# Choosing 256 keys by a threshold built bit by bit, in place of rounds of eight

## The reference

```python
def indexer_scores(qi, wi, ki):
    s = jnp.einsum('bqhd,bsd->bqhs', qi, ki).astype(jnp.float32)
    return jnp.einsum('bqhs,bqh->bqs', jax.nn.relu(s), wi.astype(jnp.float32)) * (IDX_DIM ** -0.5 * IDX_HEADS ** -0.5)

sc = jnp.where((key_chunk[None, :] <= q_chunk[:, None])[None], sc, -jnp.inf)
_, idx = lax.top_k(sc, k_sel)            # k_sel = 256 (80 for the sample)
valid = (idx // CHUNK) <= q_chunk[None, :, None]
return selected_attention(qblk, gather_rows(k, idx), gather_rows(v, idx), valid)
```

## Time and profile before

| | |
|---|---|
| time, median of 3 runs | 2787.55 us (2786.24 to 2788.78) |
| profiled execution, its span | 2790.9 us |
| PE busy | 2646.1 us (95%) |
| DVE busy | 1546.9 us (55%) |
| ACT busy | 922.8 us (33%) |
| POOL busy | 175.6 us (6%) |
| all MAX8 (202) | 170.9 us |
| all MATCH_REPLACE8 (202) | 172.1 us |

### The profile page before, as it was taken

How to read it: one execution, slowest core, us unless ns; L and a number is a source line. 1 busy time by engine, 2 the same in 40 slices (tenths; PEclk the granted TensorE clock), 3 DMA queues, 4 the chain that set the end, 5 groups by cost and what they waited for, 6 DMA issues and landing times. The chain is left out here.

```text
span 2790.9 us, 36346 instructions
## 1 busy us (share of the span) xinstructions
PE 2646.1 (95%) x14198; PEld 2323.7 (83%) x14198; DVE 1546.9 (55%) x2793; ACT 922.8 (33%) x1762; POOL 175.6 (6%) x168
## 2 busy tenths in 40 slices
PE   7999999999999999979969988899999999999996
PEld 6778789989899999868757777887898999999895
DVE  2445363444444444566889799963634444444535
ACT  3207343323222222322044555562532222223231
POOL 0300040000000000300020000000400000000003
PEclk9999999999999999989965898899999999999998
DMA  4110311101010101131100000003110101011011
GB/s 136 46 41 1 115 49 45 61 30 60 30 60 30 60 30 45 61 94 31 44 8 1 1 1 1 1 30 121 59 46 31 60 30 59 31 42 48 30 46 65
DMA packets 81279, 124.25 MB, mean 45 GB/s; under 512 B 6224, under 2 KB 54736, under 8 KB 81168
## 3 DMA queue, kind: packets, MB, share of 16 engines
q1 hardware_dynamic: 81168, 122.74, 13.4%
HBM read 110.98 MB, written 11.75 MB: 44 GB/s over the span
## 5 line engine op out<-in xcount | busy, mean ns | idle before, releaser
L1213 PE MATMUL psum<-xt_hi,layer_w_hi 128*128 128x384 f32 (+1 forms) x1536 | 505.5, 329 | 3.2 <-DVE xt_lo L847 3.2
L1215 PE MATMUL psum<-xt_hi,layer_w_lo 128*128 128x384 f32 (+1 forms) x1536 | 505.0, 329 | 0.0
L1214 PE MATMUL psum<-xt_lo,layer_w_hi 128*128 128x384 f32 (+1 forms) x1536 | 504.9, 329 | 0.0
L1128 DVE TENSOR_TENSOR act<-psum,act 128x512 f32<-128x512 f32 x540 | 366.2, 689 | 233.6 <-PE psum L1251 230.7
L1249 PE MATMUL psum<-layer_w_hi,layer_h_split 128*128 128x512 f32 x1024 | 400.0, 391 | 2.8 <-DVE layer_h_split L1116 1.6
L1250 PE MATMUL psum<-layer_w_lo,layer_h_split 128*128 128x512 f32 x1024 | 399.3, 390 | 0.0
L1251 PE MATMUL psum<-layer_w_hi,layer_h_split 128*128 128x512 f32 x1024 | 399.1, 390 | 0.0
L1116 DVE TENSOR_TENSOR layer_h_split<-layer_h_raw,layer_h_split 128x384 fp32r<-128x384 f32 (+1 forms) x192 | 98.4, 512 | 352.8 <-ACT layer_h_split L1029 352.8
L1213 PEld LDWEIGHTS psum<-xt_hi,layer_w_hi 128*128 128x128 f32 x1536 | 288.3, 188 | 4.7 <-DVE xt_lo L847 3.5
L1214 PEld LDWEIGHTS psum<-xt_lo,layer_w_hi 128*128 128x128 f32 x1536 | 288.4, 188 | 1.3
L1215 PEld LDWEIGHTS psum<-xt_hi,layer_w_lo 128*128 128x128 f32 x1536 | 288.4, 188 | 0.0
(11 more groups left out here) (215 smaller groups left out, 4067.5 us busy)
## 6 DMA issues: line engine op xcount, KB each, us to landing
layer_w_raw<-in_ff_w SPq DMA_DIRECT2D x64, 1024.0 KB, 6.3
ab_in_w_raw<-in_ab_w_in SPq DMA_DIRECT2D x12, 512.0 KB, 4.5
c_in_w_raw<-in_c_w_in SPq DMA_DIRECT2D x12, 512.0 KB, 3.9
ab_in_xt_raw<-in_xT SPq DMA_DIRECT2D x8, 512.0 KB, 4.2
layer_resid<-in_x SPq DMA_DIRECT2D x16, 256.0 KB, 2.8
x_scratch<-act SPq DMA_DIRECT2D x8, 512.0 KB, 2.6
layer_resid<-x_scratch SPq DMA_DIRECT2D x16, 256.0 KB, 2.7
out_y_prompt<-act SPq DMA_DIRECT2D x8, 512.0 KB, 2.6
```

Source lines behind the costliest of these rows:

```text
L1128: dve.tensor_tensor(acc, banks[4 + g % 4][0:r], acc, ALU.add).then_inc(y_read, 1)
L1213: pe.matmul(out, w1_hi[:, k, w], xt_hi[:, k, a:b], start=(k == 0), stop=False)
L1214: pe.matmul(out, w1_hi[:, k, w], xt_lo[:, k, a:b], start=False, stop=False)
L1215: mm = pe.matmul(out, w1_lo[:, k, w], xt_hi[:, k, a:b], start=False, stop=(k == KT - 1))
```

## The change

For tiles 7 to 2 (m = 1 to 6) the 256th largest score is found as a threshold, bit by bit from bit 30 down, and the mask is made by comparing with it. The sample keeps its rounds of eight. A first pass counts the scores that are at least 0; where a query has fewer than 256, its row's signs are flipped, so that the threshold is positive. Each of 31 further passes counts the scores at or above the threshold so far (`tensor_scalar` with `accum_out`, its elementwise output going to a spare buffer); the sign of the count's excess says whether the bit tried last stays, and two instructions on one column, bitwise ones, drop it or not and set the next bit. The tables that place the rounds are the same: 32 finds and marks for each tile at the same heads. `close` becomes longer: signs are restored, scores above the threshold are counted, those equal to it are numbered by a running sum, and as many of them as are still missing are kept. All later rounds wait for a close, which uses both spare buffers. `spare` takes 2 x 1024 fp32 per partition next to the score buffers; the program's scratch for dynamic DMA is set to 4096 in exchange. `MASKED` becomes a power of two.

```diff
-MASKED = -1e30
+MASKED = -(2.0 ** 100)
...
+def counted(m):
+
+    return C_RANKED[m] < SAMPLE
...
+        spare = top.take("ranking_spare", [P, 2, SEQ])
+        found = {m: 0 for m in range(len(C_RANKED))}
...
+    def row(self, m, n):
+
+        return self.eight(m)[:, n:n + 1]
+
+    def after(self, dve, m):
+
+        if max(self.last.get(m, 0), self.closed):
+            dve.wait_ge(self.chain, max(self.last.get(m, 0), self.closed))
+
     def find(self, dve, ranks):
 
         for m in ranks:
-            if m in self.last:
-                dve.wait_ge(self.chain, self.last[m])
-            self.step(m, dve.max(self.eight(m), self.scored(m)))
+            self.after(dve, m)
+            x = self.scored(m)
+            if not counted(m):
+                self.step(m, dve.max(self.eight(m), x))
+                continue
+            r, nk = x.shape
+            excess, short, _, threshold = [self.row(m, n) for n in range(4)]
+            ones = self.spare[0:r, m % 2, 0:nk]
+            if self.found[m] == 0:
+                self.step(m, dve.tensor_scalar(ones, x, 0.0, 0.5 - TOPK, ALU.is_ge, ALU.add, accum_out=excess))
+            else:
+                self.step(m, dve.tensor_scalar(ones, x, threshold, short, ALU.is_ge, ALU.add, accum_out=excess))
 
     def mark(self, dve, ranks):
 
         for m in ranks:
-            dve.wait_ge(self.chain, self.last[m])
-            self.step(m, dve.match_replace(self.scored(m), self.eight(m), self.scored(m), TAKEN))
+            x = self.scored(m)
+            self.after(dve, m)
+            if not counted(m):
+                self.step(m, dve.match_replace(x, self.eight(m), x, TAKEN))
+                continue
+            nk = x.shape[1]
+            excess, short, sign, threshold, dropped = [self.row(m, n) for n in range(5)]
+            if self.found[m] == 0:
+                dve.memset(threshold, 2.0)
+                self.step(m, dve.tensor_scalar(short, excess, 0.0, float(nk - 2 * TOPK + 1), ALU.is_ge, ALU.mult))
+                self.after(dve, m)
+                dve.tensor_scalar(short, short, TOPK - nk - 0.5, None, ALU.add)
+                self.step(m, dve.tensor_scalar(sign, excess, 0.0, 2.0, ALU.is_ge, ALU.mult))
+                self.after(dve, m)
+                self.step(m, dve.tensor_scalar(sign, sign, -1.0, None, ALU.add))
+                self.after(dve, m)
+                self.step(m, dve.tensor_scalar(x, x, sign, None, ALU.mult))
+            else:
+                bit = 1 << (TOP_BIT - self.found[m] + 1)
+                self.step(m, dve.tensor_scalar(dropped.bitcast(I32), excess.bitcast(I32), SIGN_SHIFT, bit,
+                                               ALU.arith_shift_right, ALU.bitwise_and))
+                self.after(dve, m)
+                self.step(m, dve.scalar_tensor_tensor(out=threshold.bitcast(I32), in0=dropped.bitcast(I32), scalar=bit >> 1,
+                                                      in1=threshold.bitcast(I32), op0=ALU.bitwise_xor, op1=ALU.bitwise_xor))
+            self.found[m] += 1
...
     def close(self, dve, m):
...
+        above, _, sign, threshold, ties = [self.row(m, n) for n in range(5)]
+        equal, nth = self.spare[0:r, 0, 0:nk], self.spare[0:r, 1, 0:nk]
+        dve.wait_ge(self.chain, self.steps)
+        dve.tensor_scalar(threshold, threshold, sign, None, ALU.mult)
+        self.step(m, dve.tensor_scalar(x, x, sign, None, ALU.mult))
+        self.after(dve, m)
+        self.step(m, dve.tensor_scalar(nth, x, threshold, None, ALU.is_gt, ALU.add, accum_out=above))
+        dve.tensor_scalar(equal, x, threshold, -MASKED, ALU.is_equal, ALU.mult)
+        self.after(dve, m)
+        self.step(m, dve.tensor_scalar(ties, above, float(TOPK), MASKED, ALU.subtract, ALU.mult))
+        self.after(dve, m)
+        self.step(m, dve.tensor_tensor_scan(nth, equal, equal, 0.0, ALU.add, ALU.bypass))
+        self.after(dve, m)
+        dve.tensor_scalar(x, x, threshold, MASKED, ALU.is_le, ALU.mult)
+        self.step(m, dve.scalar_tensor_tensor(out=nth, in0=nth, scalar=ties, in1=equal, op0=ALU.is_le, op1=ALU.mult))
+        self.after(dve, m)
+        self.step(m, dve.tensor_tensor(x, x, nth, ALU.add))
+        self.closed = self.steps
...
-    nc = bacc.Bacc("TRN2", target_bir_lowering=False, num_devices=1)
+    nc = bacc.Bacc("TRN2", target_bir_lowering=False, num_devices=1, dynamic_dma_scratch_size=4096)
```

More of the change, by code:

```diff
@@ L28 @@
 F32R = mybir.dt.float32r
+I32 = mybir.dt.int32
 P = 128
@@ L117 @@
 KEY_QUADS = [range(s0, min(s0 + 4, KEY_SLOTS)) for s0 in range(0, KEY_SLOTS, 4)]
+TOP_BIT = 30
+SIGN_SHIFT = 31
+def counted(m):
+    return C_RANKED[m] < SAMPLE
 def tok(t):
@@ L173, in encoder @@
         xt_lo = split.take("xt_lo", [P, KT, TOK], F32R)
-        top_at = (nc.sbuf_usable_end - 4 * (sum(IDX_WIDTH) + 8 * RING)) // 32 * 32
+        top_at = (nc.sbuf_usable_end - 4 * (sum(IDX_WIDTH) + 8 * RING + 2 * SEQ)) // 32 * 32
         top = Room(nc, "c_", top_at)
@@ L197, in encoder @@
         block_c_in(nc, aps, Room(nc, "c_in_", split.at, rank0_at), Room(nc, "c_in_scratch_", act_at, act_at + 4 * NT * D),
-                   A, xt_hi, xt_lo, kc, vc, ki, qi, wi, idx, top8, ident_r, x2_stored, early_c, ps)
+                   A, xt_hi, xt_lo, kc, vc, ki, qi, wi, idx, top8, spare, found, ident_r, x2_stored, early_c, ps)
         block_c_mixer(nc, Room(nc, "c_mix_", max(keep_b.at, keep_c.at), top_at - piece), A, kc, vc, ki, qi, wi, idx, top8,
-                      ident, ident_r, early_1, ps)
+                      spare, found, ident, ident_r, early_1, ps)
         block_layer(nc, aps, base.from_here("layer1_"), split.from_here("layer1w_"), 1, aps["x2"], aps["c_w_out"], A,
@@ L1327, with __init__ @@
 class Ranking:
-    def __init__(self, nc, c, tag, first, idx, top8, wi, rel, where):
+    def __init__(self, nc, c, tag, first, idx, top8, spare, found, wi, rel, where):
         self.first, self.idx, self.top8, self.wi, self.rel, self.where = first, idx, top8, wi, rel, where
+        self.spare, self.found = spare, found
         s = lambda what: c(nc.semaphore(tag + what))
@@ L1338, in __init__ @@
         self.steps = 0
+        self.closed = 0
         self.last = {}
@@ L1401, in close @@
     def close(self, dve, m):
-        dve.wait_ge(self.chain, self.last[m])
-        self.step(m, dve.tensor_scalar(self.scored(m), self.scored(m), TAKEN, MASKED, ALU.not_equal, ALU.mult))
+        x = self.scored(m)
+        self.after(dve, m)
+        if not counted(m):
+            self.step(m, dve.tensor_scalar(x, x, TAKEN, MASKED, ALU.not_equal, ALU.mult))
+            return
+        r, nk = x.shape
+        above, _, sign, threshold, ties = [self.row(m, n) for n in range(5)]
[13 more added lines that the diff above has]
+        self.step(m, dve.scalar_tensor_tensor(out=nth, in0=nth, scalar=ties, in1=equal, op0=ALU.is_le, op1=ALU.mult))
+        self.after(dve, m)
+        self.step(m, dve.tensor_tensor(x, x, nth, ALU.add))
+        self.closed = self.steps
     def product(self, pe, out, q, m, ki_hh, ki_ll):
@@ L1428, with block_c_in @@
 KEY_PARTS = [(slice(0, OWN), P), (slice(OWN, KEY_SLOTS), DEC)]
-def block_c_in(nc, aps, room, scratch, A, xt_hi, xt_lo, kc, vc, ki, qi, wi, idx, top8, ident_r, x2_stored, early, ps):
+def block_c_in(nc, aps, room, scratch, A, xt_hi, xt_lo, kc, vc, ki, qi, wi, idx, top8, spare, found, ident_r, x2_stored, early, ps):
     tag = "c_in_"
@@ L1457, in block_c_in @@
             "p b c -> p (b c)")[:, 0:nkeys(C_RANKED[m])]
-        ranking = Ranking(nc, c, tag, 0, idx, top8, wi, rel, item_out)
+        ranking = Ranking(nc, c, tag, 0, idx, top8, spare, found, wi, rel, item_out)
         ih_made, il_made = [c(nc.semaphore(tag + n)) for n in ("k_idx_hi_made", "k_idx_lo_made")]
@@ L1653, in _, with block_c_mixer @@
                         beside(t)
-def block_c_mixer(nc, room, A, kc, vc, ki, qi, wi, idx, top8, ident, ident_r, next_early, ps):
+def block_c_mixer(nc, room, A, kc, vc, ki, qi, wi, idx, top8, spare, found, ident, ident_r, next_early, ps):
     tag = "c_mix_"
@@ L1762, in block_c_mixer @@
         wide = lambda use, r, n: ps[0:r, place[use][0]:place[use][-1] + 1].rearrange("p b c -> p (b c)")[:, 0:n]
-        ranking = Ranking(nc, c, tag, RING, idx, top8, wi, rel,
+        ranking = Ranking(nc, c, tag, RING, idx, top8, spare, found, wi, rel,
                           lambda m, i: wide(("item", m, i), rows(RANKED[m]), nkeys(RANKED[m])))
```

## The result

The changed kernel takes 2793.49 us (median of 20 runs, 2789.15 to 2799.39), the kernel before 2788.4 us (20 runs, 2786.01 to 2799.49). The ratio is 1.0017, 95% interval 1.0009 to 1.0024: 0.17% slower, which is within the 0.2% that the measurement tells from no change. The forecast was 2770; 23.5 us are missing.

The account below looks back on a forecast made before the run. DVE was taken to bound tiles 0, 1, 6, 5 and 3, PE other stages; terms summed to -21.7 us, or -17.3 with the slower running sum, off the 2787.55 median: 2770 us, own range 2757 to 2784, 2735 to 2787 with rival 1.

Parts of the forecast that it names:

- What bounds the kernel: DVE bounds tiles 0, 1, 6, 5 and 3; PE bounds projection, sample and tile 2; tiles 7 and 4 are mixed.
- the price of a round: On DVE, a new round costs 1.04 ns x keys + 0.47 us, an old one 2.08 ns x keys + 0.19.
- the pair: Two rounds on DVE, for 768 and 640 keys: near 2.4 us, down from 3.31.
- the slower running sum: In closings, the running sum at half rate, 2.33 us at 1024 keys: adds 4.4 us over six tiles.
- the sum: Stage-by-stage total of expected changes: -21.7 us, or -17.3 with the running sum at half rate.
- Tiles 0 and 1: Shorter rounds on DVE save 8 us in tile 0 and 3.5 in tile 1, where PE leaves less room.
- rival 3: With DVE lighter in tiles 0 and 1, PE's clock rises earlier; sample about 36 us, kernel 2755 to 2760; chance 8%.
- PE's floor, 50 us, is far: Tile 6: DVE's savings count in full, -8.3 us, since PE's least time of 50 us does not limit it.
- each closing priced at its length on DVE: Closing at 1024 keys costs 6.8 to 7.9 us more on DVE; the next tile's first score read waits for it.
- tile 7: Rounds in its last 11 heads save 5 us, PE's floor 0.45 us per block; tile 6's closing added, +1.1.
- Rival 1: The count runs at the plain tensor_scalar's rate, 0.54 ns per key less per round: 2738 us; chance 20%.
- rival 2: The rounds' short steps eat the gain, 0.39 us or more instead of 0.27: no faster, up to 2802; chance 12%.

Follow-up runs that it names:

- filled closings: The changed kernel with unread products on PE ahead of the first transposes of tiles 7 to 2, DVE's queue unchanged: 2776.62 us.
- PE kept awake: The changed kernel with unread products at the closings and from the preparation through the sample: 2777.47 us; the kernel before with unread products, none at closings: 2797.51 us.
- second trace of the changed kernel: The changed kernel, nothing altered, executed once more for another trace: 2797.27 us, a single execution.
- split closings: The changed kernel with each closing cut into six parts behind the last six heads of the tile before, rounds ending six heads earlier: 2789.62 us.
- unread products in each head: The changed kernel with the closing cut into six parts, plus unread products on PE ahead of each head of tiles 7 to 4: 2792.05 us.

## Why the prediction was wrong

- **What bounds the kernel; the price of a round.** Right. The count costs 1.33 us at 1024 keys with both scalars from columns (forecast 1.27), the pair 2.50 us (2.4), a closing of 896 keys 7.7 us (0.6 + 6.1 + 0.9 = 7.6, with the slower running sum, which at 2.29 us for 1024 keys is the end that I took). DVE's busy time fell by 8.6 us in tile 6 and 5.2 in tile 5, which is what the sum has (7.5 and 4).
- **Tiles 0 and 1.** Right: -7.6 and -5.1 us for -8 and -3.5. In tile 1 the clock did rise (0.67), a piece of rival 3, but it fell again in the sample, which took 41.0 us in one trace and 46.6 in the other (44.2 before).
- **The step that failed: "PE's floor, 50 us, is far", with each closing priced at its length on DVE.** I forecast an idle PE after each closing and gave it no price; the floor was taken from a tile where PE is never idle. PE resumes at half speed, and then it, not DVE, sets the next two or three heads. Compared with the traces in which PE is filled (tiles 6, 4 and 3 with filled closings, tile 5, whose gap that run fills only in part, with PE kept awake as well), the first four heads take 4.4, 3.7, 3.2 and 1.4 us more in tiles 6, 5, 4 and 3: 12.7 us by direct count. By the medians, the filled closings gave back 16.9 of the 23.5 us that were missing, without touching DVE. Tiles 6 and 3 then take 70.9 and 31.8 us, within 2 us of what the sum has for them (68.9 and 31.4, the slower running sum included); tile 5, at 64.3, stays 3.8 above. In the second trace of the changed kernel each of the tiles 7 to 3 is 3.6 to 5.7 us longer than the sum. The Trainium skill, "TensorE: Matmul & The Clock Gate", section "HAM oscillation — how this bites in real kernels", has the rule that a PE left waiting is throttled again and starts the next stretch cold; the traces here agree (1.90 against 3.51 us for the same 16 products), for a wait on DVE in place of the page's wait on a DMA. It speaks against the change, and it was not weighed.
- **A second, smaller term: tile 7.** Its last heads were to come down to 0.45 us per key block, or a little above: -5 us. PE also has the next tile's queries and indexer products there, which the floor taken from tile 2 leaves out: heads 53 to 62 went from 4.49 to 4.30 us on average, with PE busy for 40.0 of their 43.0 us at clock 1.00 and DVE for 36.8. That is -1.9 in place of -5.
- **Rivals.** Rival 1 (the count at half the price) is out by 1332 ns, rival 2 (the short steps) by 0.23 us per round, rival 3 by the sample's 41.0 and 46.6 us (it had 36). The mechanism that decided was none of the three.
- **What stays open.** PE's level also falls in stretches that no closing precedes, at other places in each trace (tile 6's heads 76 to 78 in one, tile 4 and the sample in the other), and it did so before the change (tile 4 at 0.75). Which of them the change causes isn't settled; in the runs with split closings and with PE kept awake, the unread products against them cost as much as they gave. Some 3 to 4 of the 23.5 us, beside tile 7's 3.1, are not traced to a cause.

## What to carry to other kernels

Work taken off one engine and given back as one long stall is not the same work: price a stall by what the starved engine does after it, too. Here TensorE stood idle for 5 to 7 us and did the products of its next two or three heads at half speed. Products that nobody reads, given to it during such waits, brought 16.9 us; given to it in every head of four tiles, they brought nothing. A cheaper instruction is worth most if it fits where the dearer one did not, here beside a stage that TensorE bounds.

## What was not expected of the hardware

- `tensor_tensor_scan` takes twice that per key: 2292 ns at 1024 keys, 957 at 384.
- Half speed stood behind shorter waits of PE too, 2.15 to 4.45 us inside tiles 6 and 5 with the closing cut up: tile 5's granted clock was 0.83 there, against 0.89 with the closing in one piece, and 0.97 with unread products in each head.
